# Band attention in cycles of two head pairs, with 24 output matmuls in one go, in a streaming encoder layer

## The reference, cut to what matters

```python
h = einsum('bsd,de->bse', x, w_in)           # u_a, v_a, z_a, q, k, v_b, z_b, 512 columns each
u_a = gelu(...); v_a = layernorm(gelu(...))
a_out = u_a * (tril(w_s) @ v_a + b_s)        # 128-frame chunks, 4 channel groups
scores = einsum('bnqhd,bnkhd->bnhqk', qc, kb) * HEAD_DIM_B ** -0.5 + bias   # 64-frame chunks, 8 heads of 64
p = softmax(where(valid, scores, -inf))      # own chunk and the 8 before: a band of 576 keys
b_out = einsum('bnhqk,bnkhd->bnqhd', p, vb)
y = concatenate([a_out * silu(z_a), b_out * silu(z_b)])
out = layernorm(ALPHA * x + y @ w_out)
```

## Time and profile before

| | |
|---|---|
| median of 3 runs | 1087.22 us (1086.82 to 1087.52) |
| the profiled execution | 1088.48 us, its span 1086.4 us |
| granted TensorE clock | 0.999 of full speed |
| busy in the span | TensorE 1068.6, weight loads 912.4, VectorE 465.3, ScalarE 328.1, GpSimd 213.6 us |
| HBM traffic | 128 GB/s over the span |

### The profile page before, as it was taken

One profiled execution on the slowest core, in us unless ns is written; L12 is line 12 of the kernel. 1 busy time (PEld: TensorE's weight loads), 2 busy tenths in 40 slices (PEclk: granted clock), 3 DMA queues, 4 the chain that ended last, 5 costly groups with the idle time before them and its releaser, 6 DMA issues.

```text
span 1086.4 us, 17667 instructions
## 1 busy us (share of the span) xinstructions
PE 1068.6 (98%) x7338; PEld 912.4 (84%) x7338; DVE 465.3 (43%) x964; ACT 328.1 (30%) x636; POOL 213.6 (20%) x163
## 2 busy tenths in 40 slices
PE   9999999999999999999999999999999999999997
PEld 7988889999999999999999877777777777788875
DVE  6544441212212111211122024677667667777755
ACT  6410101111111111111112134454454454555530
POOL 0111112010110000000000000553443333444331
PEclk9999999999999999999999999999999999999999
DMA  9561114222211333333331454695555444444322
GB/s 339 193 182 49 39 39 129 75 86 64 75 56 54 116 136 116 113 120 112 119 124 49 126 167 136 201 285 167 147 148 167 134 139 143 135 141 142 125 88 79
DMA packets 129966, 137.33 MB, mean 126 GB/s; under 512 B 7496, under 2 KB 103904, under 8 KB 129888
## 3 DMA queue, kind: packets, MB, share of 16 engines
q1 hardware_dynamic: 124992, 121.54, 35.4%
q10 hardware_dynamic: 4896, 14.68, 4.2%
HBM read 86.62 MB, written 52.72 MB: 128 GB/s over the span
## 4 chain that ended last, share of the span: by engine, by line
PE 94%; DVE 2%; POOL 2%; DMA 1%; ACT 1%; issue 1%; POOLq 0%; DVEq 0%; SPq 0%
PE s_ps L1169 34%; PE s_ps L1186 16%; PE out_ps L1351 15%; PE pt_ps L1169 8%; PE o_ps L1328 6%; PE s_ps L1256 5%; PE pt_ps L1290 4%; PE s_ps L1351 2%; DVE prob L1057 1%; POOL wo_l L718 1%; PE o_ps L1198 1%; PE out_ps L1198 1%; DMA bias<-s_skew 1%; ACT prob L878 0%; DMA wo_raw<-w_o 0%
## 5 line engine op out<-in xcount | busy, mean ns | idle before, releaser
L1169 PE MATMUL s_ps<-xh,ring 128*128 128x512 f32 (+1 forms) x1200 | 341.3, 362 | 0.8 <-ACT st L842 0.8
L1169 PEld LDWEIGHTS s_ps<-xh,ring 128*128 128x128 f32 x1200 | 221.2, 188 | 24.6 <-issue 1.2
L1169 PE MATMUL s_ps<-xl,ring 128*128 128x512 f32 (+1 forms) x600 | 217.1, 362 | 0.0
L1186 PE MATMUL s_ps<-ring,xh 128*128 128x512 f32 x544 | 170.9, 395 | 0.0
L871 ACT ACTIVATE pt<-pt_ps 128x1024 f32<-128x1024 f32 (+3 forms) x112 | 78.9, 704 | 167.6 <-PE pt_ps L1290 167.3
L1169 PEld LDWEIGHTS s_ps<-xl,ring 128*128 128x128 f32 x600 | 112.6, 188 | 11.8
L1186 PEld LDWEIGHTS s_ps<-ring,xh 128*128 128x128 f32 x544 | 99.8, 188 | 20.2
L1186 PE MATMUL s_ps<-ring,xl 128*128 128x512 f32 x272 | 106.0, 390 | 0.0
L1038 DVE CUSTOM_DVE_ANT_1 prob<-s_ps,bias 128x640 f32<-128x640 f32 (+1 forms) x112 | 85.5, 801 | 45.8 <-PE s_ps L1256 45.7
L1351 PE MATMUL out_ps<-wo_h,yh 128*128 128x512 f32 x248 | 102.9, 415 | 0.5 <-POOL wo_l L718 0.5
L878 ACT ACTIVATE prob<-prob,low 128x640 f32<-128x640 f32 (+3 forms) x136 | 100.2, 740 | 5.1 <-DVE low L1038 4.9
(11 more groups left out here) (138 smaller groups left out, 1235.9 us busy)
## 6 DMA issues: line engine op xcount, KB each, us to landing
raw<-w_all ACTq DMA_DIRECT2D x26, 512.0 KB, 3.6
yr<-s_y SPq DMA_DIRECT2D x17, 512.0 KB, 4.8
r<-x SPq DMA_DIRECT2D x17, 512.0 KB, 3.6
q<-s_q SPq DMA_DIRECT2D x16, 512.0 KB, 4.2
k<-s_k SPq DMA_DIRECT2D x16, 512.0 KB, 5.6
y_out<-r SPq DMA_DIRECT2D x15, 512.0 KB, 3.7
s_y<-st SPq DMA_DIRECT2D x24, 256.0 KB, 2.3
x_raw<-x_t SPq DMA_DIRECT2D x12, 384.0 KB, 12.9
```

Of the source, the lines that this page charges most:

```text
L1169: last = nc.tensor.matmul(bank[b][:, 0:width], w[:, kc, :], xx[:, kc, :], start=kc == 0 and a == 0, stop=kc == KC - 1 and a == 2)
L1186: last = nc.tensor.matmul(out, xx[:, kc, cols], ring[:, 0:GRP, side, kc, :], start=kc == 0 and a == 0, stop=kc == KC - 1 and a == 2)
```

## The change

Steps become cycles, two units each. In cycle c TensorE does, in this order, the fifth block of unit 2c - 3, the scores of unit 2c, the first transposes of 2c - 2, the products with v of 2c - 3, 24 output matmuls (a whole half of an output tile; in the v phase half a v tile, and the other half at the cycle's end), the fifth block of 2c - 2, the scores of 2c + 1, the first transposes of 2c - 1 and the products with v of 2c - 2. The other engines' lists follow. With it: six buffers of probabilities for four; yr lies where yl is, so that it is loaded only when the products of the tile before last are done; z moves to the place of yr and is loaded in cycle 2; a stream's operands are put in place by ScalarE; the statistics come after the bias sums of the cycle's second unit; the last v tile is projected in one piece, and the output weights of half 1 are loaded right behind it; the stream tile is the 13th output tile and no longer the 16th. Of the loops over steps only the new form is shown (the old one stands above), and SP's is cut.

```diff
-def gate_step(tile):
-    return PLACE["pair", tile, GRP - 1] + 2
-V_STEPS = 2 * (TILES - V_EARLY)
-STEPS = V_STEPS + 4 * TILES
-ORDER = [*range(PTILES - 1), PTILES, PTILES - 1]
-START = [V_STEPS + 4 * n for n in range(TILES)]
-SPLIT = [s - 1 for s in START]
-GATED = [gate_step(t) for t in range(PTILES)] + [PLACE["stream", SB - 1, None] + 3]
-Y_LOAD = [max(START[max(n - 2, 0)] + 1 - 7 * (n < 2), GATED[ORDER[n]] + 1) for n in range(TILES)]
-X_LOAD = [V_STEPS, V_STEPS] + [START[n - 2] + 7 for n in range(2, TILES)]
+V_CYCLES = TILES - V_EARLY
+CYCLES = V_CYCLES + 2 * TILES
+ORDER = [*range(12), PTILES, *range(12, PTILES)]
+START = [V_CYCLES + 2 * n for n in range(TILES)]
+def gate_cycle(unit):
+    return (unit + 4) // 2
+GATED = [gate_cycle(PLACE["pair", t, GRP - 1]) for t in range(PTILES)] + [gate_cycle(PLACE["stream", SB - 1, None]) + 1]
+LATE = [n for n in range(TILES) if GATED[ORDER[n]] >= START[n] - 1]
+Y_LOAD = [max(START[n] - 2, GATED[ORDER[n]]) for n in range(TILES)]
+X_LOAD = [V_CYCLES, V_CYCLES] + [START[n - 2] + 3 for n in range(2, TILES)]
 POOL_TILES = TILES - TAIL
+SLOTS = 6
...
-        yr = [at(f"yr{s}", x_at[2] + 16384 + 4096 * s, [KC, P]) for s in range(2)]
+        yr = [at(f"yr{s}", x_at[3 + s] + 20480, [KC, P]) for s in range(2)]
...
-            return (HEADS_BEFORE[unit] + h) % 4
+            return (HEADS_BEFORE[unit] + h) % SLOTS
...
-                    sp.wait_ge(y_split, n - 1)
+                    sp.wait_ge(out_done, 2 * n - 2)
...
-                if step == 10:
+                if cycle == START[0] - 3:
                     sp.wait_ge(proj_done, DONE["v", 13])
                     for j in range(4):
                         load_wo(j)
-                if step == V_STEPS:
-                    sp.wait_ge(proj_done, DONE["v", TILES - 1])
-                    for j in range(4, 8):
-                        load_wo(j)
-                        if j % 2:
-                            load_x(j // 2 - 2)
+                if cycle == V_CYCLES:
                     load_keys(0)
...
+                if cycle == V_CYCLES - 1:
+                    sp.wait_ge(proj_done, DONE["v", TILES - 1])
+                    for j in range(4, 8):
+                        load_wo(j)
+                        if j % 2:
+                            load_x(j // 2 - 2)
+                    store_v(V_EARLY + cycle)
...
+            def place_stream(b):
+                at_b = slice(b * SN, b * SN + SN)
+                if b == 0:
+                    act.wait_ge(qd_zero, 1)
+                else:
+                    act.wait_ge(scored, HEADS_BEFORE[PLACE["stream", b - 1, None]] + 1)
+                nc.scalar.activation(kt[:, :, PAST:SKEYS], ks[:, :, at_b], ACT.Copy).then_inc(q_ready, 1)
+                nc.scalar.activation(qd[0:HD, :, 0:SN], qs[0:HD, :, at_b], ACT.Copy).then_inc(q_ready, 1)
+                nc.scalar.activation(qd[HD:P, :, SN:2 * SN], qs[HD:P, :, at_b], ACT.Copy).then_inc(q_ready, 1)
...
+            for cycle in range(CYCLES):
+                if is_stream(2 * cycle - 4):
+                    keep_sums(2 * cycle - 4)
+                copy_fifth(2 * cycle - 3)
+                for n in LATE:
+                    if START[n] == cycle:
+                        y_high_part(n)
+                exponents(2 * cycle - 1)
+                copy_first(2 * cycle - 2)
+                exponents(2 * cycle)
+                if 1 <= cycle < V_CYCLES:
+                    copy_v(V_EARLY + cycle - 1)
+                if is_stream(2 * cycle - 3):
+                    keep_sums(2 * cycle - 3)
+                for n in range(TILES):
+                    if START[n] - 1 == cycle and n not in LATE:
+                        y_high_part(n)
+                for unit in (2 * cycle + 2, 2 * cycle + 3):
+                    if is_stream(unit):
+                        place_stream(UNITS[unit][1])
+                copy_fifth(2 * cycle - 2)
+                copy_first(2 * cycle - 1)
+                if cycle == V_CYCLES - 1:
+                    copy_v(V_EARLY + cycle)
...
+            def statistics(n, h):
+                at_h = slice(512 * h, 512 * h + 512)
                 dve.wait_ge(out_read, 2 * n + h + 1)
...
+            for cycle in range(CYCLES):
+                if closes_tile(2 * cycle - 4):
+                    gate(UNITS[2 * cycle - 4][1])
+                if is_stream(2 * cycle - 4):
+                    gate_stream(UNITS[2 * cycle - 4][1])
+                for n in LATE:
+                    if START[n] == cycle:
+                        y_low_part(n)
+                biases(2 * cycle)
+                if closes_tile(2 * cycle - 3):
+                    gate(UNITS[2 * cycle - 3][1])
+                normalise_all(2 * cycle - 1)
+                normalise_all(2 * cycle)
+                for n in range(TILES):
+                    if START[n] - 1 == cycle and n not in LATE:
+                        y_low_part(n)
+                n, h = divmod(cycle - V_CYCLES, 2)
+                if n >= 0:
                     residual(n, h)
+                if is_stream(2 * cycle - 3):
+                    gate_stream(UNITS[2 * cycle - 3][1])
+                biases(2 * cycle + 1)
+                if n >= 0:
+                    statistics(n, h)
                     if h == 1:
                         moments(n)
                         if n >= POOL_TILES:
...
-            def quarter(step):
-                if step < V_STEPS:
-                    k0 = 4 * (step % 2)
-                    project_tile("v", V_EARLY + step // 2, k0, k0 + 4)
+            def middle(cycle):
+                if cycle < V_CYCLES:
+                    project_tile("v", V_EARLY + cycle, 0, KC if cycle == V_CYCLES - 1 else KC // 2)
                 else:
-                    n, j = divmod(step - V_STEPS, 4)
-                    project_out(n, j // 2, 4 * (j % 2), 4 * (j % 2) + 4)
+                    n, h = divmod(cycle - V_CYCLES, 2)
+                    for c0 in range(0, KC, 4):
+                        project_out(n, h, c0, c0 + 4)
...
+            for cycle in range(CYCLES):
+                turn_fifth(2 * cycle - 3)
+                score(2 * cycle)
+                if is_stream(2 * cycle - 4):
+                    turn_back(UNITS[2 * cycle - 4][1])
+                turn_first(2 * cycle - 2)
+                weigh_unit(2 * cycle - 3)
+                middle(cycle)
+                if is_stream(2 * cycle - 3):
+                    turn_back(UNITS[2 * cycle - 3][1])
+                turn_fifth(2 * cycle - 2)
+                score(2 * cycle + 1)
+                turn_first(2 * cycle - 1)
+                weigh_unit(2 * cycle - 2)
+                if cycle < V_CYCLES - 1:
+                    project_tile("v", V_EARLY + cycle, KC // 2, KC)
```

More of the change, by code:

```diff
@@ L585, in _ @@
                     load_v(1)
[L587 to L606, removed]
+            for cycle in range(CYCLES + 2):
+                for unit in (2 * cycle, 2 * cycle + 1):
+                    if opens_tile(unit):
+                        sp.wait_ge(scored, HEADS_BEFORE[unit])
+                        load_qk(UNITS[unit][1] + 1)
+                if cycle == 2:
+                    sp.wait_ge(proj_done, DONE["v", 10])
+                    load_z(0)
+                    load_z(1)
+                for unit in (2 * cycle - 4, 2 * cycle - 3):
+                    if opens_tile(unit + 1):
+                        t = UNITS[unit + 1][1]
+                        sp.wait_ge(weighed, unit + 1)
+                        if t == 1:
+                            sp.wait_ge(mix_done, TILES)
+                        if t == 3:
+                            sp.wait_ge(ya_full, GRP * NCH)
+                            sp.wait_ge(kf_stored, 16 * GRP)
+                        load_v(t + 1)
+                        sp.wait_ge(gated, t)
+                        load_z(t + 1)
+                if 1 <= cycle < V_CYCLES:
+                    store_v(V_EARLY + cycle - 1)
                 for t in range(PTILES):
-                    if GATED[t] == step:
+                    if GATED[t] == cycle:
                         sp.wait_ge(gated, t + 1)
@@ L641, in _ @@
                 for n in range(TILES):
[L642 removed]
+                    if Y_LOAD[n] == cycle:
                         load_y(n)
+                if cycle == V_CYCLES - 1:
[5 more added lines that the diff above has]
+                    store_v(V_EARLY + cycle)
                 for n in range(TILES):
[L645 removed]
+                    if START[n] + 3 == cycle and n < TILES - 2:
                         if n < POOL_TILES:
@@ L650, in _ @@
                         sp.dma_start(y_out[ORDER[n] * P:ORDER[n] * P + P, :], r[n % 2][:]).then_inc(r_stored[n % 2], 16)
-                    if n >= 2 and X_LOAD[n] == step:
+                    if n >= 2 and X_LOAD[n] == cycle:
                         load_x(n)
@@ new lines, in copy_first, with copy_fifth, exponents @@
+            def copy_first(unit):
+                if 0 <= unit < NU:
```

(23 more changed lines are left out.)

123 lines of the change are left out of this document (39 added, 84 removed).

## The result

The changed kernel takes 1090.95 us (median of 8 runs, 1088.86 to 1092.55) against 1087.64 us (1086.82 to 1088.02, 8 runs) of the kernel before: a ratio of 1.0029, 95% interval 1.0020 to 1.0038. It is slower by 3.3 us where 9 us less were forecast, and lies outside the range of 1070.5 to 1086. Its profiled execution took 1088.86 us with a span of 1086.8 us. That is the shortest of its eight, and 0.4 us above the profiled execution of the kernel before, so the two traces show only 0.4 us of the 3.3; its other executions took up to 3.7 us more.

The account below looks back on a forecast made before the run. TensorE was taken to bound the kernel, with switches between products and a few waits to save. Terms -9.5 + 2.8 + 1.0 + 4.2 - 7.7 + 0.3 + 0.2 = -8.7 us gave 1079.8, median-adjusted 1078.5; range 1070.5 to 1086 us.

Parts of the forecast that it names:

- SP queue: Loads issued by SP: load_y has 17 us for 4.8, only tile 11 is late, 0.2 us; other loads 0.
- weights: Output weights of half 1 in the opening: 1.0 us of stall against 0.7 before, +0.3 us (bounds -0.7 and 1.5).
- streams: Eight stream units on TensorE lose part of the switch saving, 0.35 us each: +2.8 us (bounds 1 and 5).
- seams: Between cycles: 0.05 us for 20, +1.0 us; after streams, four even and four odd, +4.2 us (bounds 2 and 8).
- tile 11: Its y load, gated in cycle 29 and split at the start of 30, comes late: +0.2 us.
- Switches: TensorE's changes between kinds of product: 0.34 us saved a cycle in 28 cycles, -9.5 us (bounds -5.6 and -14).
- Stalls that go: TensorE's waits behind slow scalings, stream operands, late residual and first units' bias table vanish: -7.7 us (bounds -4 and -8.5).
- rival B: GpSimd collision slows VectorE's second scaling; residual, bias sums, next scores wait: 13 tiles by 1.5 us, 1098 us; chance 0.07.
- A: Seams hold TensorE every cycle: VectorE or ScalarE 0.2 us late in 28 cycles gives back 5.6 us, 1084; chance 0.15.
- D: Switches on TensorE bring nothing, their cost returning at new seams: sum +0.8 us, 1088.0 us; chance 0.10.

Follow-up runs that it names:

- e1: Changed kernel with y of tile 1 loaded in cycle 7, right behind the last v tile's wait, ahead of the output weights: 1082.97 us, ratio 0.9959.
- e2: Changed kernel with y of tile 1 loaded in cycle 8, behind q and k, just before the streams' keys: 1082.92 us, ratio 0.9964.
- g4: Changed kernel, y of tile 1 still loaded late, its split moved from the middle of cycle 9 to the start of cycle 10: 1085.10 us, ratio 0.9978.
- e3: Kernel before with y of tile 1 loaded in step 16, behind the streams' block, instead of step 10: 1087.95 us, ratio 1.0005.
- g3: Kernel before with GpSimd's gain and offset passes cut to one column for the first 14 output tiles: 1084.51 us, ratio 0.9971.
- f3: e1 with ScalarE evacuating the last v tile ahead of its copy of unit 13's transposes: 1083.22 us, ratio 0.9960.
- f4: e1 with GpSimd's 1024-column subtraction for the output weights cut into four of 256 columns: 1088.09 us, ratio 1.0003.
- g1: e2 with f3's order and the high parts of the last two output-weight pieces made by ScalarE in cycle 8: 1085.32 us, ratio 0.9978.
- f1: e1 with the 24 output matmuls cut into two visits of 12, residual and statistics moved to the next cycle's start: 1087.01 us, ratio 0.9993.
- f2: e1 with a stream's operands put in place by VectorE, ahead of the residual, instead of ScalarE: 1100.57 us, ratio 1.0115.
- e4: Changed kernel with the store of the last v tile issued ahead of the weights of half 1: 1094.13 us, ratio 1.0061.
- g2: e1 with GpSimd's gain and offset passes cut to one column for the first 14 output tiles: 1083.63 us, ratio 0.9964.

## Why the prediction was wrong

**The step that failed** is the one called *SP queue*: "load_y waits for out_done of the tile before last ...; issued early in cycle START-2, it has 17 us for the 4.8 us that it takes", with "load_qk, load_v, keys and values keep three units or more ahead: 0". For tile 1 it is issued behind q, k and the whole of the streams' block in cycle 8, 20.0 us after the first of the weights, and takes 6.9. I had listed the moved weights and booked them by GpSimd's splitting, but had not walked SP's list behind them instruction by instruction, nor asked what stands behind y's split on ScalarE. For tile 1 it was booked at 0, and it cost 6.4 us in the trace, 8 between the medians. e1, e2 and g4 show it; e3 shows why the same lateness was free before.

With it out of the way (e1) the sum can be held against the three stretches; the forecast's terms are put where they act (0.4 us of small stalls are left out):

| stretch | forecast | e1, lag moved |
|---|---|---|
| opening: 2 cycles -0.7, stalls -2.1, weights +0.3 | -2.5 | -0.9 |
| middle: stalls -4.1; 24 cycles -8.2, streams +2.8, seams +5.1, tile 11 +0.2 | -4.2 | -3.8 |
| end: 2 cycles -0.7, stalls -1.1, seams +0.1 | -1.7 | -0.8 |

**The middle held in its sum**, but not term by term. *Switches*: 0.34 us a cycle taken less 0.05 for the seam; measured about 0.4 with the seam in it (12.0 to 12.1 less 11.63), because the scores start 0.11 to 0.15 us after the fifth transposes where I took 0.19. The 0.22 us that the prediction took from the Trainium skill (TensorE: Matmul & The Clock Gate, The mechanism), where a weight load overlaps matmuls in flight only in another row group, was a wrong use of the rule: by the kernel's loops the last of the four transposes works on rows 64 to 127 and the first score on rows 0 to 63, which are different row groups, so 0.11 to 0.15 us does not speak against it. *Streams and seams*: the timeline around two units of a tile with streams in the changed kernel has the waits that were forecast:

```profile
815.73 0.42 PE L1376 MATMUL o_ps<-vnew,pt 16*32 16x128 f32 x8
816.68 0.34 PE L1350 MATMUL pt_ps<-ident,prob 64*128 64x64 f32 x4 [0.53 <-ACT pt L888]
...
817.89 0.33 PE L1396 MATMUL o_ps<-ident,so 128*128 128x128 f32 x1
818.15 0.71 PE L1350 MATMUL pt_ps<-ident,prob 64*128 64x64 f32 x16
819.06 1.31 PE L1388 MATMUL o_ps<-pt,v 128*64 128x128 f32 x20 [0.20 <-DVE ysb L1128]
```

0.53 and 0.20 us for an even stream (0.5 and 0.2 forecast) and 0.16 to 0.24 for an odd one (0.35). Two smaller waits for ScalarE's copies come with each pair of streams, 0.21 and 0.18 us, and were not forecast. *Stalls that go*: g3, with all but the one near 851 us gone, is 3.7 us faster in the middle than the kernel before, and e1 equals g3 there. Everything else in the middle cancels, by my terms -0.1 us and measured 279.68 - 279.74 = -0.06, but in larger parts than forecast. Over the 19 cycles with streams (10 to 28) e1 takes 221.1 us against g3's 219.1, 2.0 more where my terms give 1.2; over the five plain ones behind them 58.6 against 60.6, 2.0 less where they give 1.2. That the two misses cancel is luck. So in this stretch the net gain is as large, to 0.1 us, as what the slow scalings had cost in steps.

**The opening** fell short in e1 by 1.6 us. The stalls there were to go; they moved. "Scaled probabilities are wanted a whole cycle later ... so a scaling of 2.5 us delays nothing" holds for the transposes, but in cycle 8 two slow scalings stand ahead of the residual and the bias sums, and scores wait for these: rival B's chain, with GpSimd's weight splits in the place of the layer norm. f3, f4 and g1 show that this stretch is bound in two ways at once: shorten the one wait and GpSimd's 14 us of splitting becomes the next. (The prediction has 15.1 us from the landing of the weights to the last split; its rows give 729.79 - 715.03 = 14.8, which its sum uses.)

**The end** fell short by 0.9 us. Where no scores stand between the two groups of transposes of a unit, the second waits for ScalarE's copy of the first, twice 0.6 us. From e1's timeline:

```profile
1032.94 0.34 PE L1351 MATMUL pt_ps<-ident,prob 64*128 64x64 f32 x4
1033.32 0.38 ACT L889 ACTIVATE pt<-pt_ps 128x256 f32<-128x256 f32 x1 [0.52 <-PE pt_ps L1351]
...
1033.85 0.71 PE L1351 MATMUL pt_ps<-ident,prob 64*128 64x64 f32 x16 [0.57 <-ACT pt L889]
```

The last cycles, in which units run out, were booked like all others.

Of the rivals, A and D didn't happen: a plain seam costs 0.06 us, and f1 shows the switches paid. B's chain is one that the change had avoided, as f2 shows. That f2's 17.6 us lie near B's 19 is chance: B had 1.5 us in each of 13 tiles, f2 has four streams at 3.4 to 4.8 us, low clock included, and 2.8 us near the end. That the changed kernel might lose more before tile 1 than it gains afterwards was in none of them.

The best version is e1 or e2, 0.4% faster than the kernel before and 0.7% faster than the changed one.

## What to carry to other kernels

When a buffer moves, ask for its first use as well as for its steady one: until when does what lay there live, what is issued in between on its queue, and who stands behind its consumer in a list. A wait put early in an in-order list costs what is behind it, not what it waits for: moving the consumer behind the stream's operands and three copies got back three quarters of the loss without the data coming any sooner. A term worked out for the steady cycles has to be worked out again for the first and the last ones.

## What the runs showed of the hardware

- An issue on SP takes 0.35 to 0.58 us as a rule, but behind six loads of 512 KB, a store of 256 KB and the load of q the next two took 4.13 us each, 5.96 and 3.24 in e1 (with y(1) ahead of the six), 4.64 and 3.40 in e4: some 8 to 9 us of SP's time each time. In e3, where q and k had gone out 4.4 us before the first of the weights, the two behind the same six loads took 0.72 and 0.82. What makes an issue slow was not tested. The Trainium skill (DMA: Bandwidth & Descriptors, Issuing engines are not separate DMA queues) calls the sequencer's time to initiate a DMA usually small relative to the DMA; for these issues it was not.
- After waits of TensorE of 4.4 us (changed kernel) and 4.5 us (f4) the granted clock was at the lower level for some 4.5 to 6 us of work (16 transposes 1.05 us for 0.59; 12 matmuls 5.4 us for 2.7). Shorter waits went both ways: it stayed up after 1.70 (e1), 2.1 (g4) and 2.9 us (e4), and fell after 1.85 (g2), 2.0 to 2.5 (f2, four times) and 3.2 us (g1).
- A VectorE copy of 64 columns takes 0.19 us alone and 2.37 under a GpSimd pass of 1024 columns. A GpSimd TENSOR_TENSOR of 1024 columns takes 2.4 to 2.5 us, cut in four 2.8 to 4.4.
- What is still open: why the changed kernel's other executions take up to 3.7 us more than the profiled one (e1's spread is 2.0, g4's 6.7). One way is on record for another kernel: g2's profiled execution waits 1.85 us at 718.5 where e1's waits 1.70, but its clock then falls, and from cycle 8's output matmuls to cycle 9's it takes 14.3 us instead of 12.7. That the changed kernel's executions differ in this way isn't shown.
